# Two-block network on one core: x and memory also loaded features by tokens, memory scaled on GpSimd

## What is computed

```python
for l in range(DEPTH):
    x = x + hybrid_mixer(rms_norm(x, norm_mix[l]), w_in[l], na_rpb[l], ...)
    x = x + memory_cross_attention(rms_norm(x, norm_mem_q[l]), rms_norm(mem, norm_mem_kv[l]), ...)
    x = x + conv_ffn(rms_norm(x, norm_ffn[l]), w_up[l], ...)
```

## Time and profile before

| | us |
|---|---|
| median of 3 runs | 1920.46 (1920.07 to 1920.55) |
| the profiled execution | 1920.27 |
| its span, first to last instruction | 1918.5 |
| PE busy | 1901.5 (99%) |
| DVE, ACT, POOL busy | 1434.4, 1159.0, 399.8 |
| chain that ended last | PE 89%, DVE 6%, ACT 3% |

### The profile page before, as it was taken

One profiled execution on the slowest core, in us unless ns is written; L12 is line 12 of the kernel. 1 busy time (PEld: TensorE's weight loads), 2 busy tenths in 40 slices (PEclk: granted clock), 3 DMA queues, 4 the chain that ended last, 5 costly groups with the idle time before them and its releaser, 6 DMA issues.

```text
span 1918.5 us, 30342 instructions
## 1 busy us (share of the span) xinstructions
PE 1901.5 (99%) x11612; PEld 1655.4 (86%) x11612; DVE 1434.4 (75%) x2539; ACT 1159.0 (60%) x2120; POOL 399.8 (21%) x442
## 2 busy tenths in 40 slices
PE   8999999999999999999999999999999999999999
PEld 7878998887899988888988788888888897878887
DVE  5867976577698659866786878866885687888873
ACT  6667765476676555545667555545554666756552
POOL 1110221011012104420122204411440102122430
PEclk9999999999999999999999999999999999999999
DMA  8434656544455655555553355555556544345553
GB/s 302 135 114 145 197 188 234 181 132 134 132 177 195 199 177 190 186 193 176 181 165 108 113 166 196 190 191 186 192 188 194 187 156 148 107 135 184 189 193 126
DMA packets 90689, 329.93 MB, mean 172 GB/s; under 512 B 10032, under 2 KB 10416, under 8 KB 90288
## 3 DMA queue, kind: packets, MB, share of 16 engines
q1 hardware_dynamic: 90544, 327.98, 52.3%
HBM read 326.89 MB, written 1.05 MB: 171 GB/s over the span
## 4 chain that ended last, share of the span: by engine, by line
PE 89%; DVE 6%; ACT 3%; issue 1%; DMA 1%; SPq 0%; POOL 0%; DVEq 0%; ACTq 0%
PE PS L83 86%; PE PS L86 3%; DVE WL L98 2%; DVE TMP L108 1%; ACT WH L92 1%; ACT TMP L95 1%; DVE SM L114 1%; DMA RAW<-wts 1%; DVE SM L108 0%; SPq L80 0%; DVE X L98 0%; ACT M L92 0%; DVE SM L98 0%; DVE TMP L98 0%; DVE M L108 0%
## 5 line engine op out<-in xcount | busy, mean ns | idle before, releaser
L98 DVE TENSOR_TENSOR WL<-RAW,WH 128x1024 fp32r<-128x1024 f32 (+1 forms) x609 | 760.2, 1253 | 318.4 <-ACT WH L92 313.8
L92 ACT ACTIVATE WH<-RAW 128x1024 fp32r<-128x1024 f32 (+1 forms) x609 | 640.0, 1054 | 318.8 <-PE PS L83 312.8
L83 PE MATMUL PS<-HX,WH 128*128 128x512 f32 (+1 forms) x1920 | 526.2, 344 | 3.5 <-DVE HX L108 1.6
L83 PE MATMUL PS<-WH,GX 128*128 128x512 f32 (+1 forms) x1632 | 523.6, 392 | 2.3 <-DVE X L98 1.8
L83 PE MATMUL PS<-GX,WH 128*128 128x256 f32 (+1 forms) x2176 | 455.8, 302 | 1.6 <-DVE WL L98 0.8
L83 PE MATMUL PS<-HX,WL 128*128 128x256 f32 x1488 | 417.8, 281 | 0.0
L83 PEld LDWEIGHTS PS<-HX,WH 128*128 128x128 f32 x1920 | 332.6, 189 | 50.7 <-DVE WL L98 2.8
L83 PEld LDWEIGHTS PS<-GX,WH 128*128 128x128 f32 x2176 | 351.0, 191 | 21.3 <-issue 1.2
L83 PEld LDWEIGHTS PS<-WH,GX 128*128 128x128 f32 x1632 | 305.6, 188 | 66.2 <-issue 3.4
L83 PE MATMUL PS<-GX,WL 128*128 128x256 f32 x1264 | 356.8, 282 | 0.0
L83 PE MATMUL PS<-WL,GX 128*128 128x512 f32 (+1 forms) x816 | 316.6, 388 | 0.0
(11 more groups left out here) (142 smaller groups left out, 1667.9 us busy)
## 6 DMA issues: line engine op xcount, KB each, us to landing
RAW<-wts SPq DMA_DIRECT2D x607, 512.0 KB, 4.1
M<-bias SPq DMA_DIRECT2D x4, 512.0 KB, 10.7
M<-bias SPq DMA_DIRECT2D x1, 2048.0 KB, 9.2
X<-x SPq DMA_DIRECT2D x2, 512.0 KB, 5.6
TMP<-mem SPq DMA_DIRECT2D x1, 1024.0 KB, 11.4
out<-X SPq DMA_DIRECT2D x4, 256.0 KB, 3.4
CST<-cst SPq DMA_DIRECT2D x1, 714.0 KB, 9.1
RAW<-wts SPq DMA_DIRECT2D x2, 256.0 KB, 5.9
```

The costliest lines, as they stand in the source:

```text
L83: return Issued(self.eng and self.eng.matmul(o, l, r, start=first, stop=last, skip_group_check=share))
L92: return Issued(self.eng.activation(o, i, f, scale=scale))
L98: return Issued(self.eng and self.eng.tensor_tensor(o, a, b, op))
```

## The change

- **x features by tokens.** The host also hands over `xt`, x turned, with the norm's gains in 8 columns ahead. SP loads it first, in two parts. ACT and DVE make the high and low parts straight from it; PE's 16 transposes of x go, and 8 instead of 10 warming matmuls stand ahead of the first product. x itself is loaded later, for the squares and the residual.
- **The opening's order.** `fm_four` without a turn makes, for each tile and part, first its eight matmuls with WH (which need ACT alone) and then the four with WL. Half 1 is rounded in two pieces as half 0 is. On DVE the key tiles 0 and 1 stand between the low halves 5, 6, 7; half 8 comes behind the first pair's maxima and not ahead of them.
- **The memory.** `memt`, the memory turned, is loaded to `MEMX`. The in-place norm, 16 transposes and 4 copies go. The squares are made in the fill (behind high half 11 on ACT), `memory_norm` on DVE behind low half 12; PE spreads the result by two transposes (`rbm`) ahead of gkv, DVE copies that to `RBM` behind `inverse` of head 5, and POOL multiplies MEMX by it, four operations of 128 x 512 between its divides. `tables` moves behind the divides of the first pair.
- **`memory(k)`**, on ACT and DVE and in both layers, moves back: feature tiles 0 to 3 stood with gkv, 4 to 7 with the first half of gq; now two stand with each quarter of gq.
- **DMAs.** The constants come whole behind half 5, the bias in four parts behind halves 6, 9, 11 and 13, each with its own semaphore, `mem` behind half 8, `memt` behind 10, the parameters behind 14.

```diff
+        XG = TMP[:, 0:8]
+        XT = TMP[:, 8:2056].rearrange("p (k s) -> p k s", k=KD)
+        MEMT = M[:, 8192:10240].rearrange("p (t d) -> p t d", t=2)
+        RBM = SQ[:, 1, :]
+        PARTS = (("part", 0), 0, ("part", 1), 1, 2, 2, 3, 3)
...
+                        opening = st is None
+                        if opening:
+                            piece, h = PARTS[at[0] // 4], at[0] // 8
+                            for i in range(4 * part, 4 * part + 4):
+                                ah, al, made_by = acts[i]
+                                o = (at[0] + i - 4 * part) % 8 * 128
+                                e.wait_ge(ahi, made_by)
+                                e.wait_ge(hi, piece)
+                                e.mm(ps[n], WH[:, h % HS, o:o + 128], ah, i == 0, False)
+                                e.wait_ge(alo, made_by)
+                                e.mm(ps[n], WH[:, h % HS, o:o + 128], al, False, False)
...
-                    occupy(4)
-                    e.wait_ge(id_in, 0)
-                    turn_x(("mix", 0), 0, lambda c, t: (x_in[c], 0))
-                    occupy(6)
-                    fm_four([("nq", 0, m) for m in range(4)], mix, ("mix", 0), lambda c, t: (x_in[c], 0))
-                    e.wait_ge(cst_in, 0)
+                    occupy(8)
+                    fm_four([("nq", 0, m) for m in range(4)], mix, None, None)
...
-                    for k in range(0, KD, 2):
-                        ps = take(("memt", k // 2), WHOLE)
-                        for i in range(4):
-                            t, f = i % 2, k + i // 2
-                            e.wait_ge(made, ("mem", t))
-                            m = e.turn(ps[:, i * 128:i * 128 + 128], MEMT[:, t, f * 128:f * 128 + 128], ident)
-                        m.then_inc(turned, ("memt", k // 2))
...
+                        e.wait_ge(small, "rm")
+                        put_over("rbm", [RM[:, t:t + 1].to_broadcast([128, 128]) for t in range(2)], WT + STB)
...
+                    def high_in(k):
+                        e.wait_ge(xt_in[k // 4], 0)
+                        e.act(ACT.Copy, H(0, k), XT[:, k, :], scale=XG[:, k:k + 1]).then_inc(ahi, (("mix", 0), k))
+
                     for k in range(4):
-                        high_x(("mix", 0), k, col(P_MIX + k), 0)
-                        if k == 1:
-                            e.wait_ge(first_in, 0)
-                            e.act(ACT.Copy, WH[:, 0, 0:512], RAW[:, 0, 0:512]).then_inc(hi, "first")
-                    e.wait_ge(raw[0], 0)
-                    e.act(ACT.Copy, WH[:, 0, 512:1024], RAW[:, 0, 512:1024]).then_inc(hi, 0)
-                    e.half = 1
-                    highs_to(1)
+                        high_in(k)
+                    for h in range(2):
+                        for u in range(2):
+                            e.wait_ge(first_in if h == u == 0 else raw[h], 0 if h == u == 0 else h)
+                            o = u * 512
+                            e.act(ACT.Copy, WH[:, h, o:o + 512], RAW[:, h, o:o + 512]).then_inc(hi, PARTS[2 * h + u])
+                    e.half = 2
+                    for k in range(4, 8):
+                        high_in(k)
+                    highs_to(4)
                     for c in range(2):
                         squares(("mix", 0), c, lambda c, t: (x_in[c], 0))
-                    highs_to(2)
-                    for k in range(4, 8):
-                        high_x(("mix", 0), k, col(P_MIX + k), 0)
-                    highs_to(4)
-                    e.wait_ge(mem_in, 0)
-                    for t in range(2):
-                        for c in range(2):
-                            e.wait_ge(squared)
-                            e.act(ACT.Square, junk(c), MEMT[:, t, c * 512:c * 512 + 512],
-                                  acc=SS[:, 8 + 2 * t + c:9 + 2 * t + c]).then_inc(squared, ("mem", c, t))
+                    highs_to(5)
...
+                        if L == 0 and i in (4, 5):
+                            memory_squares(i - 4)
...
-                        memory(2 * n)
-                        memory(2 * n + 1)
...
-                        if n < 2:
-                            memory(2 * n + 4)
-                            memory(2 * n + 5)
+                        memory(2 * n)
+                        memory(2 * n + 1)
...
+                    def low_in(k):
+                        e.wait_ge(ahi, (("mix", 0), k))
+                        e.stt(Lw(0, k), XT[:, k, :], XG[:, k:k + 1], H(0, k).bitcast(F32), ALU.mult, ALU.subtract).then_inc(
+                            alo, (("mix", 0), k))
...
+                        if L == 0 and i == 7:
+                            memory_norm()
...
+                        if L == 0 and n == 0:
+                            e.wait_ge(spread, "rbm")
+                            e.copy(RBM, bank("rbm")[:, 0:S]).then_inc(dout, "rbm")
...
+                    lows_to(5)
+                    rms_over(("mix", 0))
+                    e.wait_ge(dout)
+                    key_tile(0)
+                    lows_to(7)
...
+                    divide(("na", 0), 2, [256, 256])
+                    tables(0)
+                    divide(("na", 0), 4, [256, 256], 2)
+                    e.wait_ge(memt_in, 0)
+                    e.wait_ge(dout, "rbm")
+                    for q in range(4):
+                        x = MEMX[:, 2 * q:2 * q + 2, :]
+                        e.tt(x, x, RBM.unsqueeze(1).to_broadcast([128, 2, S]), ALU.mult).then_inc(scaled, ("memx", q))
+                        if q == 1:
+                            divide(("na", 0), 6, [256, 256], 4)
+                    divide(("na", 0), 8, [256, 256], 6)
+                else:
...
-            e.dma(X[:, :, 0:512], x[:, :, 0:512]).then_inc(x_in[0], 0)
-            e.dma(CST[:, 0:C_COS], cst[:, 0:C_COS]).then_inc(id_in, 0)
+            e.dma(TMP[:, 0:1032], xt[:, 0:1032]).then_inc(xt_in[0], 0)
             e.dma(RAW[:, 0, 0:512], wts[0, :, 0:512]).then_inc(first_in, 0)
             e.dma(RAW[:, 0, 512:1024], wts[0, :, 512:1024]).then_inc(raw[0], 0)
-            e.dma(X[:, :, 512:1024], x[:, :, 512:1024]).then_inc(x_in[1], 0)
             half(1)
-            half(2)
-            e.dma(PAR[:, P_CW:P_N], par[:, P_CW:P_N]).then_inc(par_in, 0)
-            e.dma(CST[:, C_COS:C_N], cst[:, C_COS:C_N]).then_inc(cst_in, 0)
-            half(3)
-            e.dma(MEMT, mem).then_inc(mem_in, 0)
-            half(4)
+            e.dma(TMP[:, 1032:2056], xt[:, 1032:2056]).then_inc(xt_in[1], 0)
+            for h in range(2, RAWS):
+                half(h)
+            for c in range(2):
+                e.dma(X[:, :, c * 512:c * 512 + 512], x[:, :, c * 512:c * 512 + 512]).then_inc(x_in[c], 0)
             for h in range(RAWS, 2 * UNITS):
                 half(h)
-                if h < RAWS + 4:
-                    q = 2 * (h - RAWS)
-                    e.dma(BIAS[:, q:q + 2, :], bias[0, :, q:q + 2, :]).then_inc(bias_in, 0)
+                if h == RAWS:
+                    e.dma(CST[:, :], cst).then_inc(cst_in, 0)
+                if h == RAWS + 3:
+                    e.dma(MEMT, mem).then_inc(mem_in, 0)
+                if h == RAWS + 5:
+                    e.dma(MEMX, memt).then_inc(memt_in, 0)
+                if h == RAWS + 9:
+                    e.dma(PAR[:, P_CW:P_N], par[:, P_CW:P_N]).then_inc(par_in, 0)
+                if h in (RAWS + 1, RAWS + 4, RAWS + 6, RAWS + 8):
+                    q = (RAWS + 1, RAWS + 4, RAWS + 6, RAWS + 8).index(h)
+                    e.dma(BIAS[:, 2 * q:2 * q + 2, :], bias[0, :, 2 * q:2 * q + 2, :]).then_inc(pair_bias_in[q], 0)
```

More of the change, by code:

```diff
@@ L143, in rest, with build @@
             pass
-def build(nc, x, mem, wts, wdt, bias, par, cst, gf, out):
+def build(nc, x, xt, mem, memt, wts, wdt, bias, par, cst, gf, out):
     with ExitStack() as ctx:
@@ L539, in fm_four @@
                             h, o = at[0] // 8, at[0] % 8 * 128
-                            e.wait_ge(lo, "first" if at[0] < 4 else h)
+                            e.wait_ge(lo, piece if opening else h)
                             e.wait_ge(low_of(made_by), made_by)
                             wh, wl = WH[:, h % HS, o:o + 128], WL[:, h % HS, o:o + 128]
-                            e.mm(ps[n], wh, ah, i == 0, False)
-                            e.mm(ps[n], wh, al, False, False)
+                            if not opening:
+                                e.mm(ps[n], wh, ah, i == 0, False)
+                                e.mm(ps[n], wh, al, False, False)
                             m = e.mm(ps[n], wl, ah, False, i == 7)
@@ L1235, in block1, with memory_squares @@
                 highs(("nk", L, 1))
-                if L == 0:
-                    for k in range(0, KD, 2):
-                        e.wait_ge(turned, ("memt", k // 2))
-                        e.act(ACT.Copy, MEMX[:, k:k + 2, :].rearrange("p k s -> p (k s)"),
-                              bank(("memt", k // 2))[:, :]).then_inc(aout, ("memt", k // 2))
```

(53 more changed lines are left out.)

64 lines of the change are left out of this document (26 added, 38 removed).

## The result

| | before | changed |
|---|---|---|
| median, 16 runs each | 1920.25 | 1922.86 |
| lowest and highest | 1917.51, 1920.55 | 1919.63, 1924.99 |
| ratio, 95% interval | | 1.0014 (1.0008 to 1.0021) |
| profiled execution, its span | 1920.27, 1918.5 | 1923.01, 1921.2 |

The changed kernel is 2.6 us slower, 0.14%, which is less than the 0.2% of the prediction: no change by its own bound, though the interval of the ratio lies above 1. 1921.9 was forecast. The spans differ by 2.7 us, and all but 0.3 of it can be followed place by place. One execution further down, of the kernel with another bank for the spread, took 3525.10 us at a mean granted clock of 0.85; it belongs to a slower state of the chip and is left out of that kernel's times.

A forecast was written before the change was run, and what follows sets the result against it. PE, busy 99%, was taken to bound the kernel, with the byte stream second in the opening. Terms -2.2 + 1.2 + 0.3 + 1.0 + 1.3 = +1.6 us on 1920.27 gave 1921.9 us; range 1916.0 to 1925.2.

The forecast's parts named there:

- The opening: Start of layer 0: without the transposes of x, PE has its first scores at 25.9, 7.5 us earlier.
- gkv: Layer 0: PE waits 4.95 us for DVE to free key tile 2's bank, starting at 51.05, not 53.23: -2.2 us.
- Rival B: Up to gkv: bytes and squares do not hold DVE, only 0.8 us of key tile 2 remain: 1917.8 us; chance 0.19.
- C: The new waits in layers 0 and 1 do not bite and the early gain stays: 1913.1 us; chance 0.15.
- Rival D: Loads ahead of gkv: memt moves at 180 GB/s, half 11 lands 3.3 us later: 1925.2 us; chance 0.10.
- The copy of the spread: Ahead of gq in layer 0: its first tile waits for DVE to copy RBM out of the bank: +1.2 us.
- POOL: Layer 0, turn of head 4's probabilities: two multiplications of MEMX by RBM stand ahead of its divide: +0.3 us.
- memory(k): Keys' turn, both layers: moved operations lengthen DVE's rotation stretch and PE waits: +1.0 us in layer 0, +1.3 in layer 1.
- The sum: Whole kernel: the terms -2.2, +1.2, +0.3, +1.0 and +1.3 give +1.6 us, so 1921.9 us.

The follow-up runs named there:

- 1.05 MB fewer ahead: The changed kernel with memt loaded behind half 14 instead of behind half 10: 1919.11 us, ratio 0.9993.
- the late start: The changed kernel with 20 instead of 8 warming matmuls ahead of the first product: 1923.12 us, ratio 1.0014.
- the one with bank 6 alone: The changed kernel with the memory's spread in the attention output's bank, copied by DVE right behind key tile 2: 1918.92 us, ratio 0.9991.

## Why the prediction was right

**The opening.** -7.5 forecast, -7.2 measured; one wait of 0.44 for low half 5 where 0.4 was forecast. The first product came at 7.21, 0.6 before its forecast, but low half 5 held PE until 23.07, and that sets the first scores.

**gkv.** The bank, the releaser and the price held: half 11 at 36.1 forecast, 35.86 measured; gkv at 51.05 forecast, 50.49 measured, the wait 3.7 and not 4.95, because PE came 0.65 later and the chain was 0.55 shorter. Other bank: no wait at gkv. 1.05 MB fewer ahead: 2.7 us earlier, one for one. Opening 2.8 later: gkv 0.46 later. That gkv "swallows" the opening was the step on which the forecast of no gain rested, and it is shown three ways. The prediction put no limit on it; the late start shows one, ACT's 2.36 us of wait ahead of half 11. Rival B, 0.8 us of wait, is refuted, C as well. Rival D had its mechanism right in kind, since half 11 does move gkv one for one, but memt moved at the full rate: half 11 landed where 413 GB/s put it. By the 358 GB/s that the Trainium skill ("DMA: Bandwidth & Descriptors", Specifications) gives as one core's limit it would have come 3.9 us after the forecast 36.1, by the prediction's estimate; this trace, of a program on one core, held 407 GB/s and disagrees.

**The copy of the spread**: +1.2 forecast, +1.2 measured (0.98 of it as idle time ahead of gq). **POOL**: +0.3 forecast, +0.36 measured; its first two multiplications took 4.35 us, not 4.0. The size was luck. The price of 2.0 each was read at another place, and the second two of the same four took 2.54, 1.27 each (last section). At that price POOL would have had head 4 divided at about 65.6, by estimate (62.13 + 2.54 + 0.94), ahead of PE at 67.1, and the term would be nothing. What makes the first two slow are DVE's two low halves beside them, which the prediction did not ask about. No run moves them apart at this place. **memory(k)**: +1.0 and +1.3 forecast, +0.9 and +1.2 measured; both gone when the pairs stand at their old places.

**What was missing: the clock.** The sum gave +1.6 and the spans differ by 2.7. With the terms as measured (-2.74, +1.22, +0.36, +0.86, +1.22) it would have been +0.92; the clock adds 1.52 and the part not followed 0.26. I forecast an idle time of 5 us for PE and priced it at 5 us, and did not ask what PE's clock does in it. All waits of PE in the trace of before are shorter than 1.6 us (the longest is 1.55), and its page shows no fall, so nothing there had a price for it; but the length of the wait, the longest of the kernel, was reason to put a bound for it into the range. The forecast came out right by its range, and by 1.0 us, partly because two errors have opposite signs: the chain was 0.55 us too long, the clock was left out.

## What to carry to other kernels

A gain ahead of a stretch is worth what the next late resource lets through. Before crediting it, follow each queue to the first point where the faster engine meets work that hangs on bytes or on another engine's queue, and see from the order which bank, buffer or copy it will need there: an added tile in a rotation of banks moves every later tile to another bank, and so to another releaser. What is added early costs bytes ahead of all that follows; load it behind what is needed first. And a wait of PE of several us can cost more than its length: fill it, or price the clock.

## What the runs showed of the hardware

- After 3.7 to 4.0 us without work PE ran at a granted clock of 0.50 (1.2 GHz) for 3 to 5 us, after 2.9 us of it for 6 us; after 1.4 and 1.6 us it did not, in the profiles of these runs. The price beyond the wait itself was 1.5 us in the changed kernel (4.56 against 3.04 for gkv's first half) and 2.8 in the one with bank 6 alone. Matmuls that nobody reads, in the wait, kept the clock at 1.00.
- POOL's products with two inputs from the on-chip buffer and DVE's low halves, which also have two there, slow each other. POOL and DVE, changed kernel:

```profile
62.13 4.35 POOL L98 TENSOR_TENSOR M<-M,SQ 128x512 f32<-128x512 f32 x2 [10.98 <-DVE SQ L111]
...
68.26 2.54 POOL L98 TENSOR_TENSOR M<-M,SQ 128x512 f32<-128x512 f32 x2
...
61.89 3.45 DVE L98 TENSOR_TENSOR WL<-RAW,WH 128x1024 fp32r<-128x1024 f32 x2
```

  With the low halves beside them two products took 4.35 us, without them 2.54. The two low halves took 3.45 us, where two took 2.4 or so alone (1.22 for one). The Trainium skill ("SBUF — State Buffer", SBUF: two separate sides) says that a DVE instruction with two inputs there and a GpSimd instruction take turns on a shared pair of ports, the later one blocked for the whole of the other. The trace agrees. The second low half, which meets a product, runs from 63.03 to 65.35, 2.32 us. The second product, which meets this low half, runs from 64.22 to 66.48, 2.26 us. Taking turns, at 1.2 for a low half and 1.27 for a product, would by estimate end them at 65.5 and 66.8. The products of 68.26 run beside DVE's maxima, of whose two large inputs one is in PSUM.
- The stream of loads held 407 to 413 GB/s on one core over 20 us, in every kernel of this study.
